# SyncE issues the last expert's down weights ahead of the reads of the first two output slots

## The chip, the cores and the metric

The kernel runs on one core of one Trainium2 chip. The metric is the device time of one execution in microseconds. A core has TensorE (PE, with its weight loads PEld), VectorE (DVE), ScalarE (ACT), GpSimd (POOL) and SyncE (SP); SP computes nothing here and issues nearly all transfers. Transfers that SP issues go through the queue that the page calls q1 (hardware_dynamic), indirect transfers that GpSimd issues through q0 (software_dynamic), and both are carried out by the same 16 DMA engines.

## What is computed

One block of a hybrid encoder on 512 tokens of width 1024, float32: a token mixer (gated delta rule and latent attention), then a mixture of experts with its residual, then a final RMSNorm. The change lies in the last part:

```
x = x + moe_ffn(rmsnorm(x, norm_ffn_w))     # top-4 of 32 experts
    gu  = xb @ w_gate_up[e] + b_gate_up[e]  # 1024 -> 2048
    act = (up + 1.0) * (gate * sigmoid(gate * 1.702))
    ye  = act @ w_down[e] + b_down[e]       # 1024 -> 1024
y = sum over the 4 selected experts of ye * softmax weight
return rmsnorm(x, norm_final_w)
```

## The kernel before

The experts are taken in order 0 to 31. For each, up to 96 token rows are gathered, multiplied by the up weights (8 MB, eight chunks of 1 MB, line 1107) and by the down weights (4 MB, four chunks of 1 MB, line 1127), and the result is scattered to the DRAM tensor `expert_rows`. TensorE takes up(n) and then down(n-1), so that the activation of expert n-1 lies beside up(n); the last down, of expert 31, follows down(30) with no up between.

The weights go through a ring of twelve SBUF buffers. SP issues the load of a chunk when TensorE has used the chunk that lay in its buffer: `up_weights` waits on `gu_used` (line 474), `down_weights` on `dn_used` (line 480). For expert 31 the first of the four down loads waits until down(30) has used its first chunk, and so on.

`expert_rows` has four rows for each token, one for each of its selected experts; slot k is the k-th of them. As the selected experts are sorted by number, the rows of slot 0 are complete once expert 28 is scattered, those of slot 1 once expert 29 is, those of slot 2 once expert 30 is, and slot 3 needs all. `early_slot(k)` (lines 536 to 541) waits for up(31) to have used the chunks whose buffers the slot is read into, waits for the scatter (`scattered`), and issues four reads of 128 tokens, 512 KB each, which raise `slot_in[k]`. Slot 3 is read at line 565, when GpSimd has seen its last scatter land (`all_rows`, line 2238), and each of its four reads has a semaphore of its own (`rows_in`).

On VectorE, after the activation of expert 31 (`activations`, `activation_columns`, line 2098), the loop over k waits for all four reads of a slot (line 2121) and adds it with its weights, four operations of 128x1024 (line 2112, through the helper at line 1523). Then come the down bias (line 2127, helper line 1520), the fourth slot, the norm and the output (`finish`, output issued by SP at line 568).

On GpSimd `scatter(n)` waits for the scatter before it, copies its indices (line 2211), waits for `ys_done` (ScalarE has copied the result of down(n) out of PSUM, line 1171) and issues three indirect transfers (line 2215).

The helper operations of VectorE are recorded by their helper's line, so line 1523 stands for the slot adds as well as for the final scaling.

Of the kernel before, what the change touches and what calls it, by code (L numbers as in the profile page):

```python
# [39 lines left out]
NE, TOPK, DE = 32, 4, 1024  # L40
# [124 lines left out]
def build(nc, x, norm_mix, a_log, dt_bias, w_cq, w_ckv, q_norm, kv_norm, w_pair, conv_w, w_qb, w_kvb,  # L165
# [3 lines left out]
    with ctx:  # L169
# [220 lines left out]
        def _(sp):  # L390
# [86 lines left out]
            def down_weights(n, e):  # L477
                for c in range(8, 12):
                    if not first(n):
                        sp.wait_ge(dn_used, 4 * n + (c - 7 - 4))  # L480
                    sp.dma_start(ring[c], w_dn_chunk(e, c)).then_inc(chunk_in[c], 16)
# [50 lines left out]
            def slot_rows(k, t):  # L532

                return y_dram[t * P * TOPK:(t + 1) * P * TOPK, :].rearrange("(p k) d -> p k d", k=TOPK)[:, k, :]

            def early_slot(k):

                sp.wait_ge(gu_used, 8 * (NE - 1) + 2 * k + 2)
                sp.wait_ge(scattered, 16 * QUADS * (NE - TOPK + 1 + k))
                for t in range(NT):  # L540
                    sp.dma_start(yin[k][:, t, :], slot_rows(k, t)).then_inc(slot_in[k], 16)

            early_slot(0)
            early_slot(1)
            down_weights(NE - 1, NE - 1)
            early_slot(2)
            sp.wait_ge(list_done, 1)
            extra = sp.value_load(lst[0:1, 2 * LIST:2 * LIST + 1], min_val=0, max_val=MAX_EXTRA)
            with sp.If(extra > 0):
# [1773 lines left out]
```

## Time and profile before

| | |
|---|---|
| median of 3 runs | 1941.96 us (1940.05 to 1943.34) |
| the profiled execution's own time | 1944.08 us |
| its span, first to last instruction | 1942.2 us |
| mean granted clock of TensorE | 0.985 |
| PE, PEld busy | 1883.3 us (97%), 859.7 us (44%) |
| DVE, ACT, POOL busy | 585.1 us (30%), 330.0 us (17%), 259.4 us (13%) |
| DMA traffic | 497.83 MB, mean 256 GB/s |

The profiled execution took 2.12 us more than the median. Positions are given in microseconds from the span's start. The busy shares are averages over the whole span; the part that the change touches is the last 60 us or so.

### The profile page before, as it was taken

The numbers are of one execution on the slowest core, as the hardware profiler recorded it, in microseconds if no ns is written. First come the engines' busy times: TensorE is split into PE (matmuls) and PEld (weight loads), VectorE is DVE, ScalarE is ACT, GpSimd is POOL, SyncE is SP. The second block draws the span as 40 slices with busy tenths as digits, with TensorE's granted clock in tenths as the row PEclk, the third lists the DMA queues.
The fourth block names the chain that finished last, engine by engine and source line by source line (L and its number), as shares of the span: only waits on it lengthen the run. The fifth ranks groups of instructions, "written<-read, shape, count | busy, mean of one in ns | idle before, by whom it ended". The sixth has DMA issues, their size and how long they took to land.

```text
span 1942.2 us, 40703 instructions
## 1 busy us (share of the span) xinstructions
PE 1883.3 (97%) x17379; PEld 859.7 (44%) x17379; DVE 585.1 (30%) x1063; ACT 330.0 (17%) x594; POOL 259.4 (13%) x305
## 2 busy tenths in 40 slices
PE   7999999999999999998999999999999999999993
PEld 4455555555555444454343443434343434434341
DVE  2463553635532111143121121212121212212126
ACT  3223423323233000121011010101010110101001
POOL 0010010000100000012121212121212212121201
PEclk9999999999999999997999999999999999999996
DMA  9211111111102322436999999999999999999995
GB/s 377 85 64 49 38 46 33 44 50 44 45 23 87 116 90 72 182 122 246 397 416 404 417 416 400 417 417 404 415 418 410 408 416 418 412 417 418 416 405 200
DMA packets 82369, 497.83 MB, mean 256 GB/s; under 512 B 14958, under 2 KB 15638, under 8 KB 28356
## 3 DMA queue, kind: packets, MB, share of 16 engines
q1 hardware_dynamic: 72692, 480.02, 62.0%
q0 software_dynamic: 9584, 16.49, 2.3%
q8 instruction: 68, 1.11, 0.2%
q14 instruction: 25, 0.20, 0.0%
HBM read 479.21 MB, written 25.64 MB: 260 GB/s over the span
## 4 chain that ended last, share of the span: by engine, by line
PE 92%; DVE 3%; DMA 1%; DVEq 1%; ACT 1%; issue 1%; another core or an unknown queue 1%; ACTq 0%; SPq 0%; POOL 0%; POOLq 0%
PE ps L1107 34%; PE ps L598 21%; PE ps L1127 17%; PE ps L593 10%; PE ps L618 2%; PE ps L817 2%; DVE arena L1523 1%; DVE arena L1520 1%; PE ps L935 1%; PE ps L930 1%; PE ps L1113 1%; PE ps L910 0%; DVE oaT L1523 0%; DMA arena<-expert_rows 0%
## 5 line engine op out<-in xcount | busy, mean ns | idle before, releaser
L1107 PE MATMUL ps<-arena 128*32 128x512 f32 x5952 | 652.4, 594 | 2.2 <-DVE pick L2085 2.2
L1107 PEld LDWEIGHTS ps<-arena 128*32 128x32 f32 x5952 | 190.6, 110 | 423.9 <-issue 418.8
L598 PE MATMUL ps<-hT,arena 128*128 128x512 f32 x768 | 350.8, 598 | 1.2 <-DVE arena L1523 0.9
L1127 PE MATMUL ps<-arena,hT 128*32 128x256 f32 x6144 | 339.4, 381 | 6.3 <-DMA arena<-in_w_dn 6.3
L1127 PEld LDWEIGHTS ps<-arena,hT 128*32 128x32 f32 x6144 | 200.6, 110 | 152.6 <-issue 27.3
L2081 DVE TENSOR_SCALAR arena<-ps 128x768 f32<-128x768 f32 x32 | 30.6, 958 | 627.0 <-PE ps L1107 627.0
L598 PEld LDWEIGHTS ps<-hT,arena 128*128 128x128 f32 x768 | 139.0, 191 | 144.3 <-issue 140.2
L2215 POOL DMA_INDIRECT expert_rows<-hT,six x96 | 97.8, 1019 | 743.2 <-ACT hT L1171 723.7
L598 PE MATMUL ps<-arena 128*128 128x512 f32 x256 | 118.5, 603 | 4.4 <-DVE arena L1520 2.2
L1171 ACT ACTIVATE hT<-arena 128x768 f32<-128x768 f32 x31 | 48.5, 1565 | 433.9 <-DMA arena<-h_rows,gix 433.9
L2203 POOL DMA_INDIRECT arena<-h_rows,gix x93 | 95.3, 1024 | 48.9 <-issue 25.2
L1171 ACT ACTIVATE arena<-ps 128x512 f32<-128x512 f32 (+4 forms) x114 | 61.4, 539 | 186.5 <-PE ps L817 99.3
L593 PE MATMUL ps<-arena 128*128 128x128 f32 (+3 forms) x352 | 84.5, 370 | 0.0
L1171 ACT ACTIVATE hT<-ps 128x768 f32<-128x768 f32 (+1 forms) x34 | 26.8, 792 | 295.8 <-PE ps L1127 284.7
L2098 DVE STREAM_TRANSPOSE hT<-arena 128x768 f32<-128x768 f32 x32 | 31.3, 978 | 145.6 <-PE ps L1127 145.5
L1520 DVE TENSOR_TENSOR arena<-arena,ps 128x128 f32<-128x128 f32 (+1 forms) x88 | 38.1, 433 | 107.4 <-PE ps L817 57.8
L598 PEld LDWEIGHTS ps<-arena 128*128 128x128 f32 x256 | 46.0, 190 | 53.3 <-issue 46.5
L1520 DVE TENSOR_TENSOR arena<-arena 128x768 f32<-128x768 f32 (+6 forms) x55 | 66.6, 1212 | 6.7 <-issue 4.6
L593 PEld LDWEIGHTS ps<-arena 128*128 128x128 f32 x352 | 52.8, 190 | 21.6 <-issue 17.3
L1475 ACT ACTIVATE arena<-arena 128x768 f32<-128x768 f32 x32 | 27.0, 843 | 192.6 <-DVE arena L2081 192.6
L1523 DVE SCALAR_TENSOR_TENSOR arena<-arena,ps 128x512 f32<-128x512 f32 x24 | 15.6, 678 | 144.2 <-PE ps L593 143.8
L1523 DVE SCALAR_TENSOR_TENSOR arena<-ps,cw,arena 128x511 f32<-128x511 f32 (+2 forms) x72 | 53.7, 746 | 9.2 <-ACT arena L1172 4.7
(243 smaller groups left out, 1249.9 us busy)
## 6 DMA issues: line engine op xcount, KB each, us to landing
arena<-in_w_gu SPq DMA_DIRECT2D x256, 1024.0 KB
arena<-in_w_dn SPq DMA_DIRECT2D x128, 1024.0 KB
arena<-in_w_pair SPq DMA_DIRECT2D x16, 1024.0 KB, 4.9
arena<-in_w_merge SPq DMA_DIRECT2D x16, 1024.0 KB, 4.9
expert_rows<-oaT SPq DMA_DIRECT2D x4, 2048.0 KB, 25.2
arena<-expert_rows SPq DMA_DIRECT2D x16, 512.0 KB, 9.6
arena<-in_x SPq DMA_DIRECT2D x8, 512.0 KB, 6.7
arena<-in_w_qb SPq DMA_DIRECT2D x4, 768.0 KB, 4.4
```

The source lines that it names most:

```text
L593: ins = pe.matmul(dst, lhsT, rhs, start=(k == 0), stop=(k == len(pairs) - 1))
L598: ins = pe.matmul(region(name)[:, cols], lhsT, rhs, start=(k == 0), stop=(k == n - 1))
L618: ins = pe.matmul(region(name)[0:m, :], w[:, k, j * P:j * P + m], hT[:, k, :], start=(k == 0), stop=(k == KD - 1))
L817: ins = pe.matmul(region(name)[p, c * CHUNK:(c + 1) * CHUNK], lhs[p, c, :], rhs[p, c, :], start=True, stop=True)
L1107: ins = pe.matmul(gu[32 * j:32 * (j + 1), g, :], columns[:, g, k, :], ring[k][:, 512 * j:512 * (j + 1)], start=(k == 0), stop=(k == KD - 1))
L1127: ins = pe.matmul(yd[32 * j:32 * (j + 1), g, 0:256], aT[:, g, 2 * c + k, :], ring[8 + c][:, D * k + 256 * j:D * k + 256 * (j + 1)], start= ...
L1171: return ac.activation(dst, src, ACT.Copy)
L1520: return dv.tensor_tensor(o, a, b, op)
L1523: return dv.scalar_tensor_tensor(out=o, in0=a, scalar=s, in1=b, op0=op0, op1=op1)
L2098: dv.transpose(aT.rearrange("p g b m -> p (g b m)"), act.rearrange("p g f -> p (g f)")).then_inc(aT_done, 1)
L2203: po.indirect_dma_start(out=xg[:, 256 * g:256 * (g + 1)], out_offset=None, in_=h2_dram.rearrange("r (j d) -> (r j) d", j=4), in_offset=bas ...
L2215: po.indirect_dma_start(out=y_dram.rearrange("r (j d) -> (r j) d", j=4), out_offset=bass.IndirectOffsetOnAxis(ap=six[:, g:g + 1], axis=0), ...
```

## The change

It moves one call: the four loads of expert 31's down weights are issued before the reads of slots 0 and 1, where they stood between slot 1 and slot 2.

```diff
-            early_slot(0)
-            early_slot(1)
             down_weights(NE - 1, NE - 1)
-            early_slot(2)
+            for k in range(TOPK - 1):
+                early_slot(k)
```

SP's program before, at the end of the expert loop. L527 closes the loop, L530 is the load of the final norm's weights, L481 the down weights, L541 the slot reads, L548 the load of the list of surplus blocks:

```order
L527 COMPARE_AND_BRANCH
L530 DMA hT<-in_norm_final 128x1024
L541 DMA arena<-expert_rows 128x1024 x8
L481 DMA arena<-in_w_dn 128x2048 x4
L541 DMA arena<-expert_rows 128x1024 x4
L548 TENSOR_LOAD lst
L548 ISA x2
```

The same place in the changed kernel, whose later lines have moved up by one:

```order
L527 COMPARE_AND_BRANCH
L530 DMA hT<-in_norm_final 128x1024
L481 DMA arena<-in_w_dn 128x2048 x4
L541 DMA arena<-expert_rows 128x1024 x12
L547 TENSOR_LOAD lst
L547 ISA x2
```

Eight reads of 512 KB (slots 0 and 1) are now behind the four down loads and directly ahead of slot 2's four. The waits inside `early_slot` and `down_weights` are the same, and no other engine's program moves.

## Rows read from the trace of the kernel before

**Rows 1.** SP's DMA issues from 1861 us: start, duration, line, transfer, count.
```profile
1861.70 0.33 SPq L530 DMA_DIRECT2D hT<-in_norm_final  x1
1867.40 14.74 SPq L541 DMA_DIRECT2D arena<-expert_rows  x8
1884.84 8.10 SPq L481 DMA_DIRECT2D arena<-in_w_dn  x4
1904.92 1.75 SPq L541 DMA_DIRECT2D arena<-expert_rows  x4
1920.56 1.76 SPq L565 DMA_DIRECT2D arena<-expert_rows  x4
```

**Rows 2.** Timeline of PE and ACT from 1880 us, idle time and its releaser in brackets.
```profile
1882.01 10.54 PE L1127 MATMUL ps<-arena,hT 128*32 128x256 f32 x192
1898.82 12.59 PE L1127 MATMUL ps<-arena,hT 128*32 128x256 f32 x192 [6.27 <-DMA arena<-in_w_dn]
...
1911.48 0.81 ACT L1171 ACTIVATE hT<-ps 128x768 f32<-128x768 f32 x1 [18.05 <-PE ps L1127]
```

**Rows 3.** Timeline of DVE from 1892 us.
```profile
1892.62 0.98 DVE L2098 STREAM_TRANSPOSE hT<-arena 128x768 f32<-128x768 f32 x1 [5.80 <-PE ps L1127]
1893.52 4.86 DVE L1523 SCALAR_TENSOR_TENSOR oaT<-arena,w 128x1024 f32<-128x1024 f32 x4
1898.50 4.87 DVE L1523 SCALAR_TENSOR_TENSOR oaT<-arena,w,oaT 128x1024 f32<-128x1024 f32 x4
1914.69 4.87 DVE L1523 SCALAR_TENSOR_TENSOR oaT<-arena,w,oaT 128x1024 f32<-128x1024 f32 x4 [11.31 <-DMA arena<-expert_rows]
1919.75 4.62 DVE L1520 TENSOR_TENSOR oaT<-oaT,ps 128x1024 f32<-128x1024 f32 x4 [0.19 <-issue]
1925.93 2.69 DVE L1523 SCALAR_TENSOR_TENSOR oaT<-arena,w,oaT 128x1024 f32<-128x1024 f32 x2 [1.57 <-issue]
```

**Rows 4.** The chain that ended last, pieces from 1894 us.
```profile
1897.20 7.66 DMA expert_rows<-hT,six
...
1906.24 8.42 DMA arena<-expert_rows
```

**Rows 5.** Timeline of POOL: scatters 29, 30 and 31.
```profile
1865.59 0.97 POOL L2215 DMA_INDIRECT expert_rows<-hT,six  x1 [0.30 <-issue]
1871.33 0.19 POOL L2211 COPY six<-obT 128x3 int32<-128x3 int32 x1 [4.77 <-DMA expert_rows<-hT,six]
1894.28 1.35 POOL L2215 DMA_INDIRECT expert_rows<-hT,six  x1 [22.76 <-ACT hT L1171]
...
1905.03 0.19 POOL L2211 COPY six<-obT 128x3 int32<-128x3 int32 x1 [5.80 <-DMA expert_rows<-hT,six]
1913.13 0.98 POOL L2215 DMA_INDIRECT expert_rows<-hT,six  x1 [7.92 <-ACT hT L1171]
```

**Rows 6.** The norm weights' load alone (line 530): issue to landing.
```profile
DMA to landing us min/median/max: 24.3/24.3/24.3
```

**Rows 7.** The last read of slot 1 alone (line 541, 1881 to 1881.5 us).
```profile
L541 SPq DMA_DIRECT2D arena<-expert_rows x1: 1673/1673/1673, 1880.5 to 1880.5; - x1
...
DMA to landing us min/median/max: 15.7/15.7/15.7
```

**Rows 8.** The mixer's 1 MB weight loads (tile in_w_pair), with little queued.
```profile
DMA to landing us min/median/max: 4.7/4.9/16.2
```

**Rows 9.** The first read of slot 3 alone (line 565).
```profile
DMA to landing us min/median/max: 3.9/3.9/3.9
```

**Rows 10.** DMA view of 1861.5 to 1870 us: packets, MB, share of 16 engines.
```profile
q0 software_dynamic: 110, 0.26, 7.8%
```

**Rows 11.** Windows: PE, PEld, DVE, ACT, POOL busy, granted clock, DMA share, GB/s.
```profile
1894.00:1896.00 2.00, 0.00 (x0) 0.00 (x0) 2.00 (x3) 0.00 (x0) 1.42 (x2) 1.00 1.00 385
1896.00:1898.00 2.00, 0.00 (x0) 0.00 (x0) 2.00 (x2) 0.00 (x0) 1.70 (x2) 0.54 1.01 420
...
1902.00:1904.00 2.00, 2.00 (x35) 1.10 (x30) 1.37 (x2) 0.00 (x0) 0.00 (x0) 0.76 0.33 123
```

**Rows 12.** DMA to landing of all twelve early slot reads (line 541).
```profile
DMA to landing us min/median/max: 4.4/12.0/21.9
```

## The prediction

> **What bounds the kernel now.** The page's averages say TensorE, 97% busy. That holds for the expert loop, but the change touches only the last 60 us, so I read that stage: first SP's issues, then PE and DVE in time, then the chain that ended last.
>
> SP's issues [rows 1]: slots 0 and 1 go out from 1867.40 to 1882.14, expert 31's down weights from 1884.84 to 1892.94, slot 2 from 1904.92, slot 3 from 1920.56. SP is free 2.7 us before the down weights go out: what holds them is their own wait, for the first quarter of down(30), which starts at 1882.01 [rows 2]. So the slot reads do not delay the issue of the down weights. They delay the landing, because they stand ahead in the queue.
>
> The queue can be followed by landings. The norm weights, issued at 1861.70, landed 24.3 us later, at 1886.0 [rows 6]. Slot 1's last read, issued at 1880.5, landed at 1896.2 [rows 7]. Between them lie eight reads, 4.19 MB in 10.2 us, 411 GB/s. The first down chunk released PE at 1898.82 [rows 2], 2.6 us behind, which is 1 MB at 403 GB/s. The last-finishing DMA engine thus works first in, first out at some 2.55 us for 1 MB and 1.27 us for a 512 KB read.
>
> PE [rows 2]: down(30) ends at 1892.55, PE waits 6.27 us for the first down chunk, and down(31) takes 12.59 us where down(30) took 10.54. The other 2.05 us is the clock: granted in full until 1896, 0.54 from there to 1898, back to full in the 1902 to 1904 stretch [rows 11]. Down(31) ends at 1911.41.
>
> The reader should now look at whether that end is waited for. DVE [rows 3] has slots 0 and 1 added by 1903.37, waits 11.31 us for slot 2's reads, and from 1914.69 on never stops for anything long: slot 2, bias, slot 3, norm. The chain [rows 4] agrees: the last transfer of scatter 30 (issued 1897.20, landed 1904.86), then slot 2's last read (issued 1906.24, landed 1914.66), then DVE. Neither down(31) nor its weights is in it after 1892.6. Down(31) leads to scatter 31 (issued from 1913.13 [rows 5]) and to slot 3's reads at 1920.56; the first of these landed at 1924.5 [rows 9], 1.4 us before DVE took it at 1925.93. That is all the slack there is, but it is on the PE side.
>
> **The change part by part.** *Down weights.* Their issue stays at 1884.84 to 1892.94, as their waits are the same. With no reads ahead, the first starts when the norm weights are in (1886.0) and lands at 1888.6 or, by a 1 MB load with little queued, 4.9 us after its issue [rows 8], 1889.7. The last is issued near 1892.6 and lands near 1897.5. PE can start when DVE's transpose ends at 1893.60 [rows 3], so at about 1893.7 in place of 1898.82: 5.1 us earlier. The gap is then 1.1 us, and in the trace the clock was still full 3.4 us into the idle time, so down(31) should take 10.54 us: another 2.05. It ends at 1904.2, **7.2 us earlier**. It needs its last quarter at 1893.7 + 3 x 2.6 = 1901.5, and 1897.5 is in time.
>
> *Behind down(31).* ScalarE's copy ends near 1905.1, scatter 31 issues from about 1906.0 (0.84 us after the copy, as in rows 2 and 5), slot 3's first read lands at about 1918.4 (7.4 us after that issue to slot 3's issue, 1913.13 to 1920.56, and 3.9 to land), or 1 to 3 us later beside a full queue. DVE wants it after 1925. Cover: the DVE chain; all 7.2 us go into this slack, which grows from 1.4 to some 5 us.
>
> *Slots 0 and 1.* Their eight issues go from 1867.40 to after 1892.94, with 0.44 us each (1.76 for four, last of [rows 1]) to 1896.5. Before, the eight took 14.74 us, with waits and a full queue in it. They are behind the down weights, so slot 0 lands at 1897.5 + 4 x 1.27 = 1902.6, plus 0.66 for scatter 30 that shares the engines (7.8% of 8.5 us [rows 10]): 1903.3. Slot 1: 1908.4. DVE, which added slot 0 from 1893.52, now idles until 1903.3; it had 11.31 us to spare, and that is the cover that gets used up. Adding costs 4.87 + 0.12 us a slot [rows 3]: slot 0 done at 1908.3, slot 1 at 1913.4.
>
> *Slot 2.* Its reads still wait for scatter 30. Scatter 29 landed 4.77 us after its last issue with a backlog of 24 us in SP's queue [rows 5, 6], scatter 30 in 5.80, so GpSimd's queue isn't held up by SP's. I take 1902.7 to 1904.9 for scatter 30, and slot 2 is issued before slot 1 is in. It follows in the queue: 1908.4 + 5.1 = 1913.5, plus up to 0.66 for scatter 31, which now falls here: **1914.1**. Before: 1914.66.
>
> The Trainium skill's page "DMA: Bandwidth & Descriptors", Rules for kernel authors, advises to issue a transfer early, compute, and wait late. That rule speaks against this change: slot reads are put off by 25 us. By it the sum would be a loss as soon as DVE's spare time is gone; here the reads are put off to just where it ends.
>
> *Sum.* DVE takes slot 2 at max(1913.4, 1914.1) in place of 1914.69: 0.6 us earlier. From there to the end, 27.5 us, nothing moves. The profiled execution took 1944.08, 2.1 above the median; its difference is applied to the median: 1941.96 - 0.6 = **1941.4 us**.
>
> *Bounds.* Best: the down weights land as fast as 4.19 MB did before, 1886.0 + 10.2 = 1896.2, scatters cost nothing, slot 0 at 1901.3; then three slots of either 5.1 us of transfer or 4.98 of DVE put the end of the wait at 1911.5, 3.2 us gained: 1938.8. Worst near case: slot 2's four reads, alone in the queue, took 5.3 us from the first landing (1904.92 + 4.4, the minimum in [rows 12], = 1909.3) to the last at 1914.66 where three intervals of 1.27 make 3.8; the last engine lags by 1.5 us. Added, 1915.6 to 1916: 1.3 lost, 1943.3. I stay near the middle, since the queue was full for 10 us where the 411 GB/s were read, which is the case here.
>
> **Rivals.** A result within 0.2% (3.9 us) can't be told from no change by a measurement of this kernel.
>
> *A, forecast: the wait moves from TensorE's weights to the slot reads* and the end of slot 2 stays where it was. For it: the chain [rows 4]. 1938.8 to 1943.3.
>
> *B: the end follows TensorE.* Then 7.2 us go through: 1934.8. Against it: slot 3's first read had landed 1.4 us before it was used, and DVE's adds can't start before the slots are in. A part of it is possible where the engines deliver faster than 411 GB/s once the backlog is gone: landing of slot 2 before 1910.8 decides for faster by over 0.2%, which asks for 10.5 MB from 1886.0 in 24.8 us, 423 GB/s with both scatters free. Time 1934.8 to 1938.
>
> *C, the other side: the reads pile up and slot 2 lands late.* Twelve reads stand in one row. Before, reads in a filled queue took a median 12.0 and up to 21.9 us [rows 12]. With slot 2's last issue at about 1904.5 and 15.7 us, slot 1's value [rows 7], it would land at 1920.2: 5.5 us lost, 1947.5. It decides from a landing after 1918.6. For it: SP's issues themselves were held up before, and scatter 30 may land later. Against it: those times had the backlog of 24 us in them [rows 6], and at 1893 only three chunks and some are left in the queue.
>
> On the same point the Trainium skill's "DMA: Bandwidth & Descriptors", Queues, rings and completion order, says that each DMA engine takes queue rows in turn, a packet at a time. By that rule scatter 30 doesn't stand behind the reads, and C loses its second leg; the 4.77 us of scatter 29 agree.
>
> *D: it doesn't do what it says*, the down weights land at 1898 still, because one engine is behind for another reason. Then the slots follow at 1898.7 or later than A has it and the time is 1942 to 1944.
>
> **How the numbers follow.** A 0.79, B 0.08, C 0.06, D 0.07. A and D lie within 0.2%: same 0.86; faster 0.08, slower 0.06. Predicted is A's 1941.4. The range takes A's bounds and a bit of the spread of the runs: 1938.8 to 1943.9; it leaves out B, C and the rim of D.
>
> **What would show it.** Right: down loads at 1884.84 as before; PE's gap before down(31) about 1.1 us, down(31) 10.5 us, at full clock; DVE's first slot add from 1903 rather than 1893.5, with two or three short waits for the slot reads in place of the one of 11.3; slot 2's add at 1913 to 1915; slot 3's reads landed 4 us or more before use; the chain without PE after 1893. Wrong: slot 2's add before 1911 or after 1918, a wait for slot 3, or a gap of PE above 3 us.

## The result, and the profile after

The changed kernel took 1945.18 us in the median (16 runs, 1942.59 to 1948.32), the kernel before, timed beside it, 1941.93 (16 runs, 1940.05 to 1946.28). The ratio is 1.0015, with a 95% interval from 1.0008 to 1.0022: 2.9 us slower, 1.6 to 4.3. The forecast was 1941.4 and a range of 1938.8 to 1943.9. A second timing (rep2_after, 11 runs) gave 1.0021 (1.0012 to 1.0030). So the loss is small and, in the first timing, below the 0.2% that the prediction had set as the limit of what can be told from no change, but both intervals lie above 1: it is real, and it has the sign opposite to the forecast gain of 0.6 us. A loss of more than 0.2% had been given a chance of 0.06.

The expert loop ahead of the change differs in length from run to run: down(30), which no part of the change touches, starts anywhere from 1878.5 to 1882.0 us in four traces of before and from 1877.0 to 1884.2 in four of the changed kernel. Positions are therefore compared from the start of down(30), here called D. In the first trace of before D is 1882.01, in the first of the changed kernel 1879.93. The stretch from D to the end of the span is called the tail.

SP's transfers in the changed kernel (timeline of SP: start, duration, line, transfer, count); lines of this kernel are one lower than in the kernel before:

```profile
1859.63 0.33 SPq L530 DMA_DIRECT2D hT<-in_norm_final  x1
1882.77 8.10 SPq L481 DMA_DIRECT2D arena<-in_w_dn  x4
1890.97 12.58 SPq L541 DMA_DIRECT2D arena<-expert_rows  x12
1915.57 1.76 SPq L564 DMA_DIRECT2D arena<-expert_rows  x4
```

Against [rows 1] the down weights are issued at the same place, D + 2.8, and the slots behind them. PE in the changed kernel, timeline:

```profile
1879.93 10.54 PE L1126 MATMUL ps<-arena,hT 128*32 128x256 f32 x192
1891.62 11.64 PE L1126 MATMUL ps<-arena,hT 128*32 128x256 f32 x192 [1.15 <-ACT hT L1170]
```

The 6.27 us of waiting for weights [rows 2] are gone; what is left is 1.15 us for the engines that free the buffers. Down(31) ends at D + 23.3 where it ended at D + 29.4 before: 6.1 us earlier. DVE, timeline:

```profile
1903.45 4.87 DVE L1522 SCALAR_TENSOR_TENSOR oaT<-arena,w 128x1024 f32<-128x1024 f32 x4 [11.93 <-DMA arena<-expert_rows]
1908.65 4.87 DVE L1522 SCALAR_TENSOR_TENSOR oaT<-arena,w,oaT 128x1024 f32<-128x1024 f32 x4 [0.33 <-DMA arena<-expert_rows]
1914.41 4.87 DVE L1522 SCALAR_TENSOR_TENSOR oaT<-arena,w,oaT 128x1024 f32<-128x1024 f32 x4 [0.88 <-DMA arena<-expert_rows]
1925.65 2.69 DVE L1522 SCALAR_TENSOR_TENSOR oaT<-arena,w,oaT 128x1024 f32<-128x1024 f32 x2 [1.57 <-issue]
```

Against [rows 3]: slot 2's add begins at D + 34.5, before at D + 32.7. From that add to the end it is 27.5 us in both kernels. So TensorE's 6 us arrive nowhere, and the end follows the slot reads. The chain that ended last says the same, with scatter 30 and slot 2's last read in it as in [rows 4]:

```profile
1894.76 6.29 DMA expert_rows<-hT,six
...
1903.12 11.26 DMA arena<-expert_rows
```

Where the transfer time went is seen in windows (PE, PEld, DVE, ACT, POOL busy, granted clock, DMA share, GB/s). First the changed kernel, D - 3.9 to D + 32:

```profile
1876.00:1880.00 4.00, 4.00 (x44) 1.23 (x40) 0.00 (x0) 0.00 (x0) 0.00 (x0) 1.00 0.46 190
1880.00:1884.00 4.00, 4.00 (x80) 2.41 (x76) 3.65 (x5) 0.84 (x1) 0.00 (x0) 1.00 0.26 65
1884.00:1888.00 4.00, 4.00 (x81) 2.42 (x76) 0.77 (x1) 0.00 (x0) 0.00 (x0) 1.00 0.90 356
...
1894.00:1896.00 2.00, 1.98 (x31) 1.04 (x24) 0.00 (x0) 0.00 (x0) 1.43 (x2) 1.00 0.91 283
1896.00:1898.00 2.00, 1.92 (x37) 1.34 (x34) 0.00 (x0) 0.00 (x0) 0.00 (x0) 1.00 0.88 305
1898.00:1902.00 4.00, 4.00 (x80) 3.41 (x76) 0.00 (x0) 0.00 (x0) 0.18 (x1) 1.00 1.04 418
...
1910.00:1912.00 2.00, 0.00 (x0) 0.00 (x0) 2.00 (x2) 0.00 (x0) 0.78 (x1) 0.74 1.03 414
```

And the kernel before, whose D is 2.1 us later:

```profile
1878.00:1882.00 4.00, 4.00 (x40) 1.17 (x36) 0.00 (x0) 0.00 (x0) 0.00 (x0) 1.00 1.01 385
1882.00:1886.00 4.00, 4.00 (x80) 2.44 (x76) 3.57 (x5) 0.84 (x1) 0.00 (x0) 1.00 0.98 367
...
1902.00:1904.00 2.00, 2.00 (x35) 1.10 (x30) 1.37 (x2) 0.00 (x0) 0.00 (x0) 0.76 0.33 123
1904.00:1906.00 2.00, 2.00 (x44) 1.22 (x39) 0.00 (x0) 0.00 (x0) 0.19 (x1) 1.00 0.21 68
```

Before the change, slots 0 and 1 were moved around D, in a time in which no weight load can be issued, since it waits for down(30). Now the engines run dry there (190 and 65 GB/s), and the 4.2 MB of these slots are moved behind the down weights, in the same row with slot 2. Before, the dry time came late (123 and 68 GB/s), while SP waited for scatter 30.

### The profile page after: what moved, and what is told of

It is laid out like the page before. It is cut to its first block, busy times and chain, and to the rows that moved or that the text cites. A ratio compares the mean times of both kernels' runs of the same rounds, so it can differ in the third digit from the quotient of the medians.

```text
span 1941.9 us, 40703 instructions
## 1 busy us (share of the span) xinstructions
PE 1879.5 (97%) x17379; PEld 858.6 (44%) x17379; DVE 584.9 (30%) x1063; ACT 329.9 (17%) x594; POOL 260.5 (13%) x305
## 4 chain that ended last, share of the span: by engine, by line
PE 91%; DVE 3%; DMA 1%; DVEq 1%; SPq 1%; issue 1%; ACT 1%; another core or an unknown queue 1%; ACTq 0%; POOL 0%; POOLq 0%
PE ps L1106 34%; PE ps L597 21%; PE ps L1126 17%; PE ps L592 10%; PE ps L617 2%; PE ps L816 2%; DVE arena L1522 1%; DVE arena L1519 1%; PE ps L934 1%; PE ps L929 1%; DMA arena<-expert_rows 1%; PE ps L1112 1%; PE ps L909 0%; DVE oaT L1522 0%
## 5 line engine op out<-in xcount | busy, mean ns | idle before, releaser
L1170 ACT ACTIVATE arena<-ps 128x512 f32<-128x512 f32 (+4 forms) x114 | 61.5, 539 | 186.5 <-PE ps L816 99.3
## 6 DMA issues: line engine op xcount, KB each, us to landing
arena<-in_w_gu SPq DMA_DIRECT2D x256, 1024.0 KB, 16.3
```

The costliest lines, as they stand in the source:

```text
L1170: return ac.activation(dst, src, ACT.Copy)
```

## The experiments

Theory T: without these reads the DMA engines have little to move around D (the dry time), and the reads moved out of that time push slot 2's landing, which VectorE waits for; all of the loss lies behind D. Rivals: L, a part is lost ahead of D; S, slot reads behind the down weights cost by themselves (they meet scatter 30), whatever the queue holds. All positions in this table are microseconds behind D.

| kernel | down(31) starts | slot 2's add begins | end of span | ratio to before (95%) |
|---|---|---|---|---|
| before, four traces | 16.8, 16.7, 16.5, 16.5 | 32.7, 31.8, 31.9, 32.1 | 60.2, 59.3, 59.4, 59.5 | 1 |
| changed, four traces | 11.7 | 34.5, 34.5, 34.5, 34.5 | 62.0, 61.9, 62.0, 62.0 | 1.0015 (1.0008 to 1.0022), 1.0021 (1.0012 to 1.0030) |
| e1_slot0_first | 11.7 | 31.8 | 59.3 | 1.0010 (1.0000 to 1.0019) |
| e2_no_reads01 | 11.7 | 26.7 | 54.2 | 0.9980 (0.9970 to 0.9991) |
| e3_tiles_before | 16.3 | 26.5 | 58.2 | 0.9993 (0.9984 to 1.0002) |
| e4_tiles_after | 11.7 | behind slot 1's | 61.1 | 1.0012 (1.0003 to 1.0021) |
| e5_tiles_slot0 | 11.7 | behind slot 1's | 58.0 | 0.9994 (0.9985 to 1.0003) |
| e6_tiles12_bias | 11.7 | 32.1 | 54.7 | 0.9974 (0.9963 to 0.9984) |
| e7_tiles_all_after | 11.7 | 31.0 | 58.9 | 0.9996 (0.9987 to 1.0005) |
| e8_act_queue | 17.6 | 35.0 | 62.5 | 1.0010 (1.0001 to 1.0019) |
| e10_slot0_from_x | 11.7 | 34.0 | 61.5 | not timed |
| e11_slot0_pitch | 11.7 | 34.6 | 62.1 | not timed |

**Second to fourth traces of both kernels** (rep_before, rep_after, rep2_after, rep3_before, rep4_before, rep3_after).

> The kernel before, unchanged, for a second trace. Measured in each trace from the start of down(30): in the first one slot 2's add began 32.7 us behind it and the span ended 60.2 us behind it; in the changed kernel 34.5 and 62.0. If the time is lost in the tail (theory T), this trace gives 32.7 and 60.2 again within 0.5 us. If it is lost in the expert loop or earlier (rival L), the start of down(30) moves between the two kernels and the tails agree once several traces are compared.

> The changed kernel, unchanged, for a second trace. Theory T: slot 2's add 34.5 us and the end 62.0 us behind the start of down(30), within 0.5 us. Rival L: these numbers come near the 32.7 and 60.2 of the kernel before, and down(30) starts later than there by some 2 to 3 us.

> The changed kernel once more, timed. In two traces of each kernel its tail (start of down(30) to the end) was 61.9 to 62.0 us against 59.3 and 60.2. Theory T: the tail is all, ratio 1.0011 (2.2 us), tail 62 again. Rival L (a part is lost before down(30)): ratio 1.002 or more with the same tail.

> A third trace of the kernel before. The changed kernel's timed ratio is 1.0015 and 1.0021 (2.9 and 4.1 us), its tail from the start of down(30) only 2.2 us longer than the mean of two traces of before (60.2, 59.3), and these two differ by 0.9 in the landing of slot 2. If all is in the tail (theory T), before's usual tail is nearer 59 than 60; if a part is lost before down(30) (rival L), it is 59.3 to 60.2 again.

> A fourth trace of the kernel before, for the same question: theory T a tail of 58.5 to 59.3, rival L 59.3 to 60.2.

> A fourth trace of the changed kernel: its three tails so far are 61.9 to 62.0. Theory T needs them to be 62 or more as a rule, rival L asks for a later start of down(30) than in the kernel before, on the same chip, by 1 us or more.

The changed kernel repeats its tail within 0.1 us. The kernel before has 59.3 to 59.5 in three traces and 60.2 in the one that the prediction was made from: there slot 2's last read landed 0.6 to 0.9 us later than in the others. The tails differ by 61.97 - 59.6 = 2.4 us, a ratio of 1.0012, which lies in the first timed interval and on the lower edge of the second. The difference behind D is shown; that it is all of the loss is not. Against T's expectations, rep_before's tail was 0.9 us shorter than asked, rep2_after gave a ratio above 1.002 with the same tail, which was L's sign, and rep4_before's 59.5 lies in L's interval. Against L, down(30) started no later in rep3_after (1877.0) than in the kernel before on the same chip (1878.5 and 1879.9). Each kernel's D ranges over 3.5 us or more, so a further loss ahead of D of up to a microsecond or two can't be excluded; the 2.4 us behind D cover most of the measured 2.9 and 4.1.

**Slot 0 ahead of the down weights** (e1_slot0_first). The diff is against the changed kernel.

```diff
+            early_slot(0)
             down_weights(NE - 1, NE - 1)
-            for k in range(TOPK - 1):
-                early_slot(k)
+            early_slot(1)
+            early_slot(2)
```

> Slot 0 is read ahead of the down weights, slot 1 behind. Theory T (the transfer queue runs dry ahead of the down weights, because these wait for down(30), and the 4.2 MB moved behind them push slot 2's landing out): slot 0's 2.1 MB fill the dry time, the first down chunk lands about when DVE's transpose is done, so PE waits 1 to 2 us, and slot 2's add begins 31 to 32.5 us behind the start of down(30), 2 to 3.5 us sooner than in the changed kernel: 1.5 to 3 us below it in time, 1940 to 1942 us. Rival S (slot reads that are issued behind the down weights collide with scatter 30, whatever the queue holds): slot 1 and 2 are still there, slot 2's add stays at 34 or more and the time at 1944 to 1945.

DVE's timeline, D is 1881.31:

```profile
1892.82 4.86 DVE L1523 SCALAR_TENSOR_TENSOR oaT<-arena,w 128x1024 f32<-128x1024 f32 x4
1906.57 4.92 DVE L1523 SCALAR_TENSOR_TENSOR oaT<-arena,w,oaT 128x1024 f32<-128x1024 f32 x4 [8.89 <-DMA arena<-expert_rows]
1913.14 4.87 DVE L1523 SCALAR_TENSOR_TENSOR oaT<-arena,w,oaT 128x1024 f32<-128x1024 f32 x4 [1.65 <-DMA arena<-expert_rows]
```

Slot 2's add is at D + 31.8, 2.7 us sooner than in the changed kernel, and PE still starts down(31) at D + 11.7. One slot fills the dry time and costs the down weights nothing; two slots made them late, none leaves the time unused. That is T's forecast and against S. The time itself settles nothing: the ratio 1.0010 is some 2 us above what the tail says (59.3 against 59.6 would be no change), and its interval, 1.0000 to 1.0019, holds no change as well as the changed kernel's 1.0015. This is open.

**Slots 0 and 1 not read** (e2_no_reads01): VectorE adds what lies in the buffers, so the sum is another one. The diff is against the changed kernel.

```diff
             down_weights(NE - 1, NE - 1)
-            for k in range(TOPK - 1):
-                early_slot(k)
+            early_slot(2)
...
-                dv.wait_ge(slot_in[k], 16 * NT)
+                if k == 2:
+                    dv.wait_ge(slot_in[k], 16 * NT)
```

> The order of the changed kernel, with the reads of slots 0 and 1 left out (VectorE adds what lies in their buffers), so that only slot 2 is read behind the down weights. Theory T: slot 2's reads are issued when scatter 30 has landed, 20 to 21.5 us behind the start of down(30), and land alone in 9.8 us, so slot 2's add begins at 30 to 31 us and the end comes 3.5 to 4.5 us sooner than in the changed kernel: about 1941 us. Rival S (the scatter and its wait, not the queue, sets slot 2): the add stays within 1 us of 34.5, and the time within 1 us of 1945.

D is 1880.00; timelines of SP and DVE:

```profile
1898.55 1.82 SPq L541 DMA_DIRECT2D arena<-expert_rows  x4
...
1906.70 4.87 DVE L1521 SCALAR_TENSOR_TENSOR oaT<-arena,w,oaT 128x1024 f32<-128x1024 f32 x4 [5.33 <-DMA arena<-expert_rows]
```

Slot 2 is issued at D + 18.6 (scatter 30 lands 2.6 us sooner than in the changed kernel) and is in 8.15 us later. The add is 7.8 us sooner, T had said 3.5 to 4.5. The direction is T's, the size was missed: T had scatter 30 land at D + 20 to 21.5 as in the changed kernel, so the eight reads had also made the scatter late, and it had 9.8 us for slot 2's transfer, which took 8.15. The end is 7.8 us sooner too, and PE's weights had no part in that, as down(31) starts at D + 11.7 in both.

**A semaphore for each read of slot 2**, in three orders (e3_tiles_before, e4_tiles_after, e5_tiles_slot0, the last with e1's order).

```diff
-                    sp.dma_start(yin[k][:, t, :], slot_rows(k, t)).then_inc(slot_in[k], 16)
+                    sp.dma_start(yin[k][:, t, :], slot_rows(k, t)).then_inc(w_in[t] if k == 2 else slot_in[k], 16)
...
-                dv.wait_ge(slot_in[k], 16 * NT)
-                add_slot(k)
+                if k < 2:
+                    dv.wait_ge(slot_in[k], 16 * NT)
+                for t in range(NT):
+                    if k == 2:
+                        dv.wait_ge(w_in[t], 16 * 8 + 16)
+                    add_rows(k, t)
+                dv.drain()
```

> The order of the kernel before; slot 2's four reads have a semaphore each, and VectorE adds each 128 tokens when their own read is in, not when all four are. In the two traces of before, slot 2's add begins 32.7 and 31.8 us behind the start of down(30) and the end is at 60.2 and 59.3. Theory T (VectorE waits for slot reads; TensorE's down(31) leads only to slot 3's reads, which had 1.4 us to spare): slot 2 is added by 34 instead of 37.6, and then slot 3's first read, at 42.5, becomes the wait, since down(31) is late in this order. Gain only the 1.4 us of slack, end at 58 to 58.8, time 1 to 2 us below before. Rival P (the end follows VectorE alone): 3.6 us gained.

DVE's timeline, D is 1876.38:

```profile
1902.83 2.57 DVE L1523 SCALAR_TENSOR_TENSOR oaT<-arena,w,oaT 128x1024 f32<-128x1024 f32 x2 [5.08 <-DMA arena<-expert_rows]
1906.93 2.54 DVE L1523 SCALAR_TENSOR_TENSOR oaT<-arena,w,oaT 128x1024 f32<-128x1024 f32 x2 [1.54 <-DMA arena<-expert_rows]
1909.67 4.62 DVE L1520 TENSOR_TENSOR oaT<-oaT,ps 128x1024 f32<-128x1024 f32 x4 [0.19 <-issue]
1918.41 2.69 DVE L1523 SCALAR_TENSOR_TENSOR oaT<-arena,w,oaT 128x1024 f32<-128x1024 f32 x2 [4.13 <-DMA arena<-expert_rows]
```

As T said: slot 2 is added by D + 33.1, and then DVE waits 4.13 us for slot 3, whose reads hang on the late down(31). The end at 58.2 is 1.4 us before the usual 59.6, which is the slack, and not the 3.6 us of rival P. Here TensorE's lateness costs something. The timed ratio, 0.9993 (0.9984 to 1.0002), has the same size and can't tell it from no change.

> The same finer wait in the order of the changed kernel. Its last slot 2 read lands 34.4 us behind the start of down(30), slot 3's first read at 39.5, well before VectorE wants it at 42. Theory T: the full 3.6 us are gained here, end at 58.2 to 58.7 in place of 61.95, time 3 to 4 us below the changed kernel, thus about that of before or 1 us less. If slot 3's reads were the bound in this order too, less than 2 us.

Missed: 61.1 in place of 58.2 to 58.7. DVE, D is 1881.44:

```profile
1904.80 4.90 DVE L1522 SCALAR_TENSOR_TENSOR oaT<-arena,w 128x1024 f32<-128x1024 f32 x4 [11.77 <-DMA arena<-expert_rows]
1910.01 9.86 DVE L1522 SCALAR_TENSOR_TENSOR oaT<-arena,w,oaT 128x1024 f32<-128x1024 f32 x8 [0.30 <-DMA arena<-expert_rows]
```

DVE starts at D + 23.4 and works through. It needs 15 us for three slots, so with slot 0 in that late DVE itself holds the end, and finer waits on slot 2 can't help. The prediction's "cover that gets used up" was used up to the last microsecond.

> Slot 0 ahead of the down weights, slots 1 and 2 behind (as in e1_slot0_first, whose slot 2 add began at 31.8 and whose end was at 59.3), with the finer wait. Theory T: both gains go together, as down(31) starts 1.1 us behind down(30) and slot 3 is in at about 37: slot 2 added by 33, end at 55.5 to 56, time 3.5 to 4.5 us below before, ratio near 0.998. Rival S (slot reads behind the down weights cost by themselves): end above 57.5.

Missed: 58.0 lies where rival S had been put. The traces give the reason of e4 in its place: slot 1 is in as a whole only at D + 25.5, and two slots in one piece (9.86 us) follow; e6_tiles12_bias below, with slots 1 and 2 still behind the down weights, ends at 54.7, which S excluded. The end here is 1.6 us before the kernel before's, and 0.9994 (0.9985 to 1.0003) can't tell it from no change.

**A semaphore for each read of all slots in the changed order** (e7_tiles_all_after). The diff is that of e4_tiles_after with four semaphores more for slots 0 and 1 each, in a table `tile_in`:

```diff
-                dv.wait_ge(slot_in[k], 16 * NT)
-                add_slot(k)
+                if k not in (0, 1, 2):
+                    dv.wait_ge(slot_in[k], 16 * NT)
+                for t in range(NT):
+                    if k in (0, 1, 2):
+                        dv.wait_ge(tile_in[k][t][0], tile_in[k][t][1] + 16)
+                    add_rows(k, t)
+                dv.drain()
```

> The changed kernel's order with a semaphore for each read of all three slots. In e4_tiles_after only slot 2 had them, and VectorE, which could start with slot 0 only when all of it was in at 23.4, then worked without a stop until 38.4: the late start had become the bound. If that reading is right, here it starts at about 19, follows the landings, has slot 2 added by 36 and ends at 58 to 59 (e4: 61.06, changed kernel: 61.95). If slot 2's landing had been later in e4 for another reason, it stays above 60.

58.9, as expected. D is 1881.59, and DVE starts at D + 17.8 and follows the landings:

```profile
1899.38 1.29 DVE L1526 SCALAR_TENSOR_TENSOR oaT<-arena,w 128x1024 f32<-128x1024 f32 x1 [6.20 <-DMA arena<-expert_rows]
1902.75 2.48 DVE L1526 SCALAR_TENSOR_TENSOR oaT<-arena,w 128x1024 f32<-128x1024 f32 x2 [2.08 <-DMA arena<-expert_rows]
...
1914.12 3.83 DVE L1526 SCALAR_TENSOR_TENSOR oaT<-arena,w,oaT 128x1024 f32<-128x1024 f32 x3 [0.28 <-DMA arena<-expert_rows]
```

**Both, and the bias in the gap** (e6_tiles12_bias): e1's order, a semaphore for each read of slots 1 and 2, and the down bias added ahead of slot 2.

```diff
             for k in range(TOPK - 1):
...
+                if k == 2:
+                    for t in range(NT):
+                        ready(dv, f"bo{t}_0", f"bo{t}_1")
+                        tt(acc[:, t, :], acc[:, t, :], banks(f"bo{t}"), ALU.add)
+                    dv.drain()
...
-            for t in range(NT):
-                ready(dv, f"bo{t}_0", f"bo{t}_1")
-                tt(acc[:, t, :], acc[:, t, :], banks(f"bo{t}"), ALU.add)
-            dv.drain()
```

> Slot 0 ahead of the down weights, 1 and 2 behind; a semaphore for each read of slots 1 and 2; and the down bias is added before slot 2 instead of behind it, in time in which VectorE waits. Theory T (VectorE, fed by the slot reads, sets the end, and TensorE has been early enough since its weights come in time): slot 1 added 27 us behind the start of down(30), bias by 32, slot 2 by 36.6, then slot 3, whose first read lands at about 37.7; end at 54 to 55, 5 us less than the 59.7 of before, ratio 0.997 to 0.998. Rival S (slots behind the down weights cost by themselves, or slot 3 is late here): end above 56.5.

D is 1884.46:

```profile
1905.34 2.63 DVE L1527 SCALAR_TENSOR_TENSOR oaT<-arena,w,oaT 128x1024 f32<-128x1024 f32 x2 [4.51 <-DMA arena<-expert_rows]
1909.06 2.57 DVE L1527 SCALAR_TENSOR_TENSOR oaT<-arena,w,oaT 128x1024 f32<-128x1024 f32 x2 [1.09 <-DMA arena<-expert_rows]
1911.81 4.62 DVE L1524 TENSOR_TENSOR oaT<-oaT,ps 128x1024 f32<-128x1024 f32 x4 [0.18 <-issue]
1916.51 4.87 DVE L1527 SCALAR_TENSOR_TENSOR oaT<-arena,w,oaT 128x1024 f32<-128x1024 f32 x4
```

End at 54.7, 5 us less than before, ratio 0.9974 (0.9963 to 0.9984): this beats both kernels. The bias is now taken at D + 27.4, when down(31) is done; in the kernel before PE finished down(31) at D + 29.4 [rows 2], so there the bias would have had to wait. No run has this order of adds without the early down(31).

**Slots 0 and 1 on ScalarE's queue** (e8_act_queue).

```diff
-            early_slot(0)
-            early_slot(1)
             down_weights(NE - 1, NE - 1)
...
+            for k in range(2):
+                ac.wait_ge(gu_used, 8 * (NE - 1) + 2 * k + 2)
+                ac.wait_ge(scattered, 16 * QUADS * (NE - TOPK + 1 + k))
+                for t in range(NT):
+                    ac.dma_start(yin[k][:, t, :], y_dram[t * P * TOPK:(t + 1) * P * TOPK, :].rearrange("(p k) d -> p k d", k=TOPK)[:, k, :]).then_inc(slot_in[k], 16)
             expert(NE - 1, False)
```

> Slots 0 and 1 are issued by ScalarE on its own queue, ahead of the activation of expert 31, so as early as in the kernel before, and SP's queue has the down weights without reads ahead. Theory T (what counts is DMA work that is done in the dry time before the down weights are issued): the slots are in before VectorE wants them at 11.5 us, the first down chunk is in time, PE's gap before down(31) is 1.1 to 2 us, slot 2's reads run alone, end at 57.5 to 60. What it may cost: the reads take turns with the weights of up(31) and down(30), which are still queued, so PE may wait up to 5 us there. Rival Q (one order of arrival for both queues): down(31) starts 16.7 us behind down(30) as in the kernel before.

Missed by both T and Q. PE's timeline, D is 1883.87:

```profile
1883.87 2.80 PE L1125 MATMUL ps<-arena,hT 128*32 128x256 f32 x48 [0.32 <-DMA arena<-in_w_dn]
1887.57 2.80 PE L1125 MATMUL ps<-arena,hT 128*32 128x256 f32 x48 [0.90 <-DMA arena<-in_w_dn]
1891.33 2.80 PE L1125 MATMUL ps<-arena,hT 128*32 128x256 f32 x48 [0.96 <-DMA arena<-in_w_dn]
...
1901.44 12.04 PE L1125 MATMUL ps<-arena,hT 128*32 128x256 f32 x192 [3.56 <-DMA arena<-in_w_dn]
```

The reads, issued from 1868.74, take turns with the weights of down(30), which were issued 6 to 14 us before them: all four quarters of down(30) now wait, and down(31) waits 3.56 us. The cost that had been put at up to 5 us is there, the gain isn't: down(31) starts at D + 17.6 and the end is at 62.5. The reads on the second queue did not wait behind these loads; the norm weights landed 34.5 us after their issue, 24.3 before [rows 6]. That agrees with the page "DMA: Bandwidth & Descriptors" of the Trainium skill, Queues, rings and completion order, by which a DMA engine takes the queue rows in turn.

**The source of slot 0's reads** (e10_slot0_from_x, e11_slot0_pitch). The sum is another one in both: slot 0 is taken from the input, or from expert 0's gate and up weights. The diff shown is that of e10.

```diff
-                    sp.dma_start(yin[k][:, t, :], slot_rows(k, t)).then_inc(slot_in[k], 16)
+                    sp.dma_start(yin[k][:, t, :], slot_rows(k, t) if k else x[t * P:(t + 1) * P, :]).then_inc(slot_in[k], 16)
```

> The changed kernel, but slot 0's four reads take adjacent 4 KB rows of the input x in place of the rows of expert_rows, which lie 16 KB apart and in the tensor that scatter 30 is writing (the output is another sum). In the traces of the changed kernel slot 0's add begins 22.8 to 23.7 us behind the start of down(30), where I had forecast 21.3, and the DMA engines moved only some 290 GB/s for 4 us at the step from weights to slot reads. If the source of the reads is the reason (pitch, or the writes beside them), slot 0's add begins at 22.0 or sooner and the 4 us show over 350 GB/s. If it is the step itself in SP's queue, 22.8 to 23.7 again.

> The same with rows that lie 16 KB apart, of the gate and up weights of expert 0, a tensor that nothing writes. If the pitch is the reason: 22.8 to 23.7 here and 22.0 in e10_slot0_from_x. If it is the scatter's writes: 22.0 or sooner in both. If it is the step in the queue: 22.8 to 23.7 in both.

The 4 us at the step from weights to slot reads (D + 14 to D + 18), first with adjacent rows, then with rows 16 KB apart in a tensor that nothing writes, last the second trace of the changed kernel (rep_after):

```profile
1895.00:1899.00 4.00, 3.55 (x58) 2.00 (x50) 0.00 (x0) 0.00 (x0) 1.50 (x2) 1.00 0.98 377
```

```profile
1895.20:1899.20 4.00, 3.20 (x58) 2.20 (x54) 0.00 (x0) 0.00 (x0) 1.56 (x2) 1.00 0.90 293
```

```profile
1896.80:1900.80 4.00, 3.93 (x67) 2.24 (x60) 0.00 (x0) 0.00 (x0) 1.46 (x2) 1.00 0.92 287
```

Adjacent rows keep the rate, 377 GB/s; rows 16 KB apart lose it with and without the scatter's writes, 287 and 293. So in these traces it is the pitch, and neither the scatter nor the step in the queue alone; for adjacent rows there is one trace. In place of 377 it costs 4 x (377 - 287) / 377 = 1.0 us.

By the start of slot 0's add the two runs would have decided nothing: D + 22.3 with adjacent rows, where 22.0 had been asked, and 22.6 with the pitch, where 22.8 to 23.7 had been. The reason is the last of the 64 parts in which the slot lands (four reads, 16 DMA engines, one semaphore increment each). Counted in the traces of the changed kernel, 63 parts are in by D + 22.4 to 22.8, and the last at D + 22.7, 23.5, 23.5 and 23.7; in e11 both are in at 22.6. In e10 all but the last of the recorded parts are in by D + 21.4, 1.0 us or more sooner, and the last at D + 22.3. Of the 1.0 us, 0.9 us reach slot 1's add (D + 27.8), but only 0.5 us slot 2's (D + 34.0).

Why the pitch costs only at the start is open: from 1898 to 1908 the changed kernel moved 408 to 421 GB/s. Nor does every such step cost as much: slot 1's reads behind the down weights moved 302 GB/s in the same 4 us in e1_slot0_first and 353 in e6_tiles12_bias.

## Why the prediction was wrong

**What bounds the end**: right. The chain was slot reads and VectorE, TensorE's weights were not in it, and the 6 us that TensorE won went into slack: slot 3's first read landed 3.9 us after its issue at 1915.57, at 1919.5, 6.2 us before DVE took it at 1925.65 (the forecast was some 5). Nothing of rival B showed, and nothing of rival D: the down weights did not land late.

**Down weights and down(31)**: right in place. The first down chunk was in time, the gap was 1.15 us for 1.1, the granted clock stayed 1.00. Down(31) took 11.64 us for a forecast 10.54; the other three traces of the changed kernel have 11.5, 12.0 and 10.57, that of e1 10.57. Where it took longer, TensorE did fewer matmuls around D + 15.3 to 16.5, at full clock, which is when the DMA rate is lowest too; but e10, which kept its rate, also took 12.0 us. The cause is open, and it is off the path.

**Slots 0 and 1**: this step failed, by the size of one term. "Slot 0 lands at 1897.5 + 4 x 1.27 = 1902.6, plus 0.66 for scatter 30: 1903.3" is D + 21.3. The add began at D + 23.5 (22.8 to 23.7 in four traces), 2.2 us late; slot 1's add at D + 28.7 and slot 2's at D + 34.5 then kept this distance (forecast 26.4 and 32.1). That step took 1.27 us a read from a time when the last engine worked off a long backlog. The term "4 x 1.27 + 0.66" = 5.7 us was too small, not the 1897.5 before it (D + 15.5; the last recorded parts of the down weights landed at D + 15.1 to 15.9). Slot 0 took 8.0 us from there. About 1 us of the 2.2 is the slow start of the reads with their 16 KB pitch (286 GB/s from D + 14 to D + 18), by e10 and e11. About another 1 us is the last single part: in the first trace 63 of 64 were in by D + 22.5 and the last at D + 23.5. The prediction had seen such a lag, 1.5 us in slot 2 of the kernel before, and put it in the range alone; its worst case for slot 2, 1916 or D + 34.0, was passed by 0.5 us. Among the signs it named "two or three short waits" of DVE, but its own sum had DVE idle for 9.7 us before slot 0; measured were 11.93 us.

**The reference point**: the 32.7 us at which slot 2's add began in the one trace of before were high; three further traces have 31.8 to 32.1. The forecast gain of 0.6 us was the difference of two numbers of over 30 us, of which one was some 0.8 above the usual 31.9. With that the sum would have been no change even with the forecast landing times.

**The sum**: 34.5 - 32.1 = 2.4 us later, against the mean of the four traces of before, in place of 0.6 us earlier. The remaining 0.5 to 1.7 us of the timed ratios are open.

**Issue early, wait late**: this rule of the Trainium skill ("DMA: Bandwidth & Descriptors", Rules for kernel authors), which the prediction set against the change, was right on the sign. In these runs putting a transfer off cost something when it left a time in which the DMA engines had nothing else to do: two slots put off cost 2.4 us in the tail, one slot (e1) nothing there. **Rival C** had the sign, but neither its size nor its reasons: the reads took 7.3 to 14.1 us to land, median 10.4, which is no more than before (4.4 to 21.9, median 12.0 [rows 12]), and scatter 30 landed at D + 21.1, sooner than before (D + 22.9).

## What to carry to other kernels

A transfer that stands ahead of an urgent one may be filling a time in which the urgent one can't be issued yet. Ask for both: what has to wait behind it, and what the DMA engines do at its old place once it is gone; here one slot of the two fits into that time without making the down weights or slot 2 late. Before a wait is removed, follow what its engine releases: TensorE's 6 us led only to slot 3, which had time. And take the duration of a transfer from a stretch in the same state (backlog, pitch), and a forecast of half a microsecond never from one trace.

## What the runs showed of the hardware

- In the 4 us around the step from contiguous weights to reads of 4 KB rows that lie 16 KB apart in DRAM, the DMA engines moved 282 to 293 GB/s (four traces of the changed kernel and e11), with adjacent rows 377 (e10, one trace). With one slot's reads ahead of the weights it was 302 (e1) and 353 (e6).
- A read is in when the last of its 16 parts is: slot 0's 64th part landed 0.3 to 1.0 us behind the 63rd in the four traces of the changed kernel.
- Reads on a second issuing queue took transfer time from weight loads issued 6 to 14 us before them, and all four loads came late (e8_act_queue).
- GpSimd's instructions that issue indirect transfers take 0.97 us, and some of them up to 2.1 us while VectorE is adding, though not all (scatter 30's second took 0.97 between two longer). Scatter 30's third, in the kernel before with VectorE adding [rows 3] and in the changed kernel with VectorE idle (timelines of POOL):

```profile
1897.20 2.02 POOL L2215 DMA_INDIRECT expert_rows<-hT,six  x1 [0.30 <-issue]
```

```profile
1894.76 0.98 POOL L2214 DMA_INDIRECT expert_rows<-hT,six  x1 [0.30 <-issue]
```

  Scatter 30 landed 1.7 us sooner in the changed kernel.
- TensorE's granted clock stayed 1.00 through the 1.15 us gap and through down(31) in the changed kernel; in the kernel before it fell to 0.54 in the 6.27 us gap, from 1896 to 1898 [rows 11].
